# Expert weights fetched in whole halves again, the residual's home exchanged, and the combine weights turned large ones first

## What is computed

```
for layer in range(2):
    mix = ab_mixer(x) if layer == 0 else hgrn_mixer(x)
    x = layer_norm(ALPHA * x + mix)
    ff = moe(x, router_w, router_bias, w_gate[layer], w_up[layer], w_down[layer])
    x = layer_norm(ALPHA * x + ff)

def moe(h, ...):          # 16 experts in 4 groups of 4; each token takes 2 of one group
    ...
    for e in range(16):
        he = silu(t @ w_gate[e]) * (t @ w_up[e])         # 1024 -> 512
        y = y + gates[:, e:e + 1] * (he @ w_down[e])     # 512 -> 1024
```

## Time and profile before

| | us |
|---|---|
| median of 3 runs | 958.73 (956.76 to 959.33) |
| the profiled execution's own time | 956.18 |
| its span, first to last instruction | 954.4 |
| PE busy | 910.4 (95%) |
| MoE of layer 0, gate of quad 0 to the end of the last down | 303 to 516 |
| MoE of layer 1, the same | 725 to 936 |

### The profile page before, as it was taken

One profiled execution on the slowest core, in us unless ns is written; L12 is line 12 of the kernel. 1 busy time (PEld: TensorE's weight loads), 2 busy tenths in 40 slices (PEclk: granted clock), 3 DMA queues, 4 the chain that ended last, 5 costly groups with the idle time before them and its releaser, 6 DMA issues.

```text
span 954.4 us, 15651 instructions
## 1 busy us (share of the span) xinstructions
PE 910.4 (95%) x6463; PEld 560.7 (59%) x6463; DVE 370.7 (39%) x955; ACT 278.4 (29%) x591; POOL 103.6 (11%) x166
## 2 busy tenths in 40 slices
PE   9999999899999999999988899999999999999885
PEld 6777877686886353434324787777875444434223
DVE  2358876955317020111303336665346120203114
ACT  3534533222005020101002248887223201001003
POOL 2222121553000000000000001111300000000000
PEclk9999999999999999999999999999999999999988
DMA  9953353995985999999993954545798999999971
GB/s 378 352 234 138 139 199 132 394 376 192 423 365 207 376 370 420 421 419 420 422 421 141 384 234 161 183 185 200 285 425 311 411 386 420 421 421 421 420 314 47
DMA packets 41309, 299.84 MB, mean 314 GB/s; under 512 B 5065, under 2 KB 6601, under 8 KB 12809
## 3 DMA queue, kind: packets, MB, share of 16 engines
q1 hardware_dynamic: 36000, 268.52, 69.7%
q0 software_dynamic: 4544, 29.65, 8.1%
q10 hardware_dynamic: 688, 0.60, 0.2%
HBM read 283.32 MB, written 15.53 MB: 313 GB/s over the span
## 4 chain that ended last, share of the span: by engine, by line
PE 76%; DMA 11%; DVE 7%; ACT 2%; issue 2%; SPq 1%; POOL 1%; ACTq 0%; DVEq 0%; POOLq 0%
PE bank L1306 20%; PE bank L1344 11%; PE bank L1494 8%; PE bank L934 7%; PE bank L1181 6%; PE bank L1481 5%; PE bank L1370 3%; DMA ring<-in_w_down 3%; PE bank L1290 3%; DMA A<-in_w_down 3%; PE bank L1202 3%; DMA W<-in_conv_cols 1%; DVE ring L2209 1%; DMA spread<-xd_rows 1%; DMA spread<-v_rows 1%
## 5 line engine op out<-in xcount | busy, mean ns | idle before, releaser
L1306 PE MATMUL bank<-ring,W 128*32 128x512 f32 x1312 | 199.7, 608 | 9.4 <-DMA ring<-in_w_up 9.4
L934 PE MATMUL bank<-xT,ring 128*128 128x264 f32 x704 | 164.0, 389 | 1.3 <-DMA ring<-in_w_ab 1.2
L934 PEld LDWEIGHTS bank<-xT,ring 128*128 128x128 f32 x704 | 131.3, 190 | 31.0 <-issue 8.0
L1306 PE MATMUL bank<-A,W 128*32 128x512 f32 x544 | 125.6, 593 | 0.0
L1306 PEld LDWEIGHTS bank<-ring,W 128*32 128x32 f32 x1312 | 54.7, 112 | 106.9 <-issue 94.0
L1344 PE MATMUL bank<-ring,A 128*32 128x512 f32 x640 | 99.6, 599 | 0.0
L1344 PE MATMUL bank<-A 128*32 128x512 f32 x336 | 87.5, 621 | 2.8 <-DMA ring<-in_w_down 2.8
L2482 DVE TENSOR_TENSOR gkg<-gkg,bank 128x512 f32<-128x512 f32 x16 | 11.0, 688 | 186.1 <-PE bank L1306 186.1
L1494 PE MATMUL bank<-xT,ring 128*128 128x264 f32 x320 | 78.0, 391 | 0.0
L1494 PEld LDWEIGHTS bank<-xT,ring 128*128 128x128 f32 x320 | 58.3, 190 | 11.1 <-issue 1.6
L1306 PEld LDWEIGHTS bank<-A,W 128*32 128x32 f32 x544 | 32.9, 110 | 45.9 <-issue 45.5
(11 more groups left out here) (340 smaller groups left out, 1218.2 us busy)
## 6 DMA issues: line engine op xcount, KB each, us to landing
ring<-in_w_up SPq DMA_DIRECT2D x42, 1024.0 KB, 20.9
ring<-in_w_down SPq DMA_DIRECT2D x38, 1024.0 KB, 19.5
ring<-in_w_gate SPq DMA_DIRECT2D x34, 1024.0 KB, 15.8
ring<-in_w_ab SPq DMA_DIRECT2D x10, 2048.0 KB, 8.9
A<-in_w_gate SPq DMA_DIRECT2D x19, 1024.0 KB, 18.9
A<-in_w_down SPq DMA_DIRECT2D x16, 1024.0 KB, 23.9
ring<-in_w_c SPq DMA_DIRECT2D x8, 2048.0 KB, 11.0
A<-in_w_up SPq DMA_DIRECT2D x14, 1024.0 KB, 16.1
```

Source lines behind the costliest of these rows:

```text
L934: mm = pe.matmul(ab_bank(m)[:, 0:T], slot(AB_IN0 + m // 4, 8)[:, c, (m % 4) * P:(m % 4 + 1) * P], xT[:, c, :], start=(c == 0), stop=(c == ...
L1306: mm = pe.matmul(out[ROWS * g:ROWS * (g + 1), :], xg[:, c, E_G * b + g, :], w[g][:, c % 4, :], start=(c == 0), stop=(c == DC - 1))
```

## The change

Three edits. First, halves 20 to 27 are fetched whole, and PE goes through the gate of quad 0 as through every other: all four chunks of a half for block 0, then for block 1, and one mark at the end of each half. Second, home 18 now holds half 19 (down half 0 of quad 0) in place of half 14; half 14 goes to the home that half 16 had, 16 to that of 17, 17 to that of 18 and 18 to that of 19. The first fetches follow the homes' order as before. ACT therefore writes the residual after down half 0 has been read, between its two copies into `Y`. Third, `turn_weights` makes its eight large products one behind the other and then the eight small ones.

```diff
-        FIRST_ORDER = [[14, 15] + list(range(14)) + list(range(16, 20)),
-                       list(range(7)) + [14, 15] + list(range(7, 14)) + list(range(16, 20))]
+        FIRST_ORDER = [[19, 15] + list(range(15)) + list(range(16, 19)),
+                       list(range(7)) + [19, 15] + list(range(7, 15)) + list(range(16, 19))]
-        FIRST_HOMES = [r[:14] + [XACC_HOME, Y_HOME] + r[14:] for r in REST_HOMES]
+        FIRST_HOMES = [r[:15] + [Y_HOME] + r[15:] + [XACC_HOME] for r in REST_HOMES]
-        SPLIT_FILLS = 8
-        FILL_PARTS = [2 if FIRST <= 4 * n < FIRST + SPLIT_FILLS else 1 for n in range(MOE_HALVES // 4)]
-        READ_MARKS = MOE_HALVES // 4 + 2
+        READ_MARKS = MOE_HALVES // 4
...
-                for k0 in range(FIRST, MOE_HALVES, 4):
-                    parts = FILL_PARTS[k0 // 4]
-                    for part in range(parts):
-                        for k in range(k0, k0 + 4):
-                            before = max(m for m in range(k) if HOMES[layer][m] == HOMES[layer][k])
-                            sp.wait_ge(sem("moe_read"), half_read(layer, before, part if parts > 1 else 1))
-                            fill_part(layer, k, part, parts)
+                for k in range(FIRST, MOE_HALVES):
+                    before = max(m for m in range(k) if HOMES[layer][m] == HOMES[layer][k])
+                    sp.wait_ge(sem("moe_read"), half_read(layer, before))
+                    fill_half(layer, k)
...
-                        if q == i == 0:
-                            for part in range(2):
-                                for b in range(2):
-                                    if b == 1 and half == part == 0:
-                                        pe.wait_ge(sem("moe_slots"), 2 * layer + 2)
-                                    for c in range(4 * half + 2 * part, 4 * half + 2 * part + 2):
-                                        mm = product(b, c)
-                                mm.then_inc(sem("moe_read"), 1)
-                        else:
-                            for b in range(2):
-                                for c in range(4 * half, 4 * half + 4):
-                                    mm = product(b, c)
-                            mm.then_inc(sem("moe_read"), 1)
+                        for b in range(2):
...
+                            for c in range(4 * half, 4 * half + 4):
...
+                        mm.then_inc(sem("moe_read"), 1)
...
                 def turn_weights():
...
                     for r in range(2 * QUADS):
-                        out = bank[(4, 5, 2)[r // 3]][:, (r % 3) * SPREAD_N:(r % 3 + 1) * SPREAD_N]
-                        pe.transpose(out[:, 0:P], WS[:, r * P:(r + 1) * P], ident[:, :])
-                        tr = pe.transpose(out[:, P:SPREAD_N], WS2[:, r * P:(r + 1) * P], ident[0:NB, 0:NB])
+                        pe.transpose(turned[r][:, 0:P], WS[:, r * P:(r + 1) * P], ident[:, :])
+                    for r in range(2 * QUADS):
+                        tr = pe.transpose(turned[r][:, P:SPREAD_N], WS2[:, r * P:(r + 1) * P], ident[0:NB, 0:NB])
                     tr.then_inc(sem("pt_turned"), 1)
...
+                        if q == i == 0:
+                            act.wait_ge(sem("moe_read"), halves_read(layer, 0, 2, 0))
+                            act.activation(xacc[:, :, :], xT[:, :, :], ACT.Copy, scale=ALPHA).then_inc(sem("moe_residual"), 1)
...
-                    if q == 0:
-                        act.wait_ge(sem("moe_read"), halves_read(layer, 0, 1, 1))
-                        act.activation(xacc[:, :, :], xT[:, :, :], ACT.Copy, scale=ALPHA).then_inc(sem("moe_residual"), 1)
```

More of the change, by code:

```diff
@@ L239, in expert_ready, with halves_read, half_read @@
             n = 6 * q + 2 * i + half
-            parts = layer * sum(FILL_PARTS[n % FILLS::FILLS]) + sum(FILL_PARTS[n % FILLS:n + 1:FILLS])
-            eng.wait_ge(sem(f"moe_filled{n % FILLS}"), 64 * parts)
-        def halves_read(layer, q, i, half, part=1):
-            if q == i == 0:
-                return READ_MARKS * layer + 2 * half + part + 1
-            return READ_MARKS * layer + 6 * q + 2 * i + half + 3
-        def half_read(layer, k, part=1):
+            eng.wait_ge(sem(f"moe_filled{n % FILLS}"), 64 * (READ_MARKS // FILLS * layer + n // FILLS + 1))
+        def halves_read(layer, q, i, half):
+            return READ_MARKS * layer + 6 * q + 2 * i + half + 1
+        def half_read(layer, k):
             q, r = divmod(k, QUAD_HALVES)
-            return halves_read(layer, q, r // 8, r % 8 // 4, part)
+            return halves_read(layer, q, r // 8, r % 8 // 4)
         slot = chunks
@@ L408, in home_free, with fill_half @@
                 return [("heads_gated", 12), ("heads_prompt_state_stored0", 16 * 6), ("heads_prompt_state_stored1", 16 * 6)]
-            def fill_part(layer, k, part, parts):
+            def fill_half(layer, k):
                 q, r = divmod(k, QUAD_HALVES)
@@ L414, in fill_part @@
                 half, g = divmod(r, 4)
-                n, at = 6 * q + 2 * i + half, HALF_W // parts * part
                 src = expert_views(layer, bass.ds(E_G * g + q, 1))[i]
-                sp.dma_start(home_of(HOMES[layer][k])[:, at:at + HALF_W // parts],
-                             src[:, HALF_W * half + at:HALF_W * half + at + HALF_W // parts]).then_inc(
-                    sem(f"moe_filled{n % FILLS}"), 16)
+                sp.dma_start(home_of(HOMES[layer][k]), src[:, HALF_W * half:HALF_W * (half + 1)]).then_inc(
+                    sem(f"moe_filled{(6 * q + 2 * i + half) % FILLS}"), 16)
             def fill_first_expert(layer, k):
@@ L424, in fill_first_expert @@
                     sp.wait_ge(sem(name), value)
-                fill_part(layer, k, 0, 1)
+                fill_half(layer, k)
             def fill_experts(layer):
@@ L1299, in gate_up @@
                         w = [expert_half(layer, q, i, half, g) for g in range(E_G)]
-                        def product(b, c):
+                        for b in range(2):
                             out = up_bank(b) if i else gate_bank(b)
[L1303 to L1308, removed]
-                                mm.then_inc(sem("block_done"), 1)
-                            return mm
@@ L1312, in gate_up @@
-                        if q == i == 0:
-                            for part in range(2):
-                                for b in range(2):
-                                    if b == 1 and half == part == 0:
-                                        pe.wait_ge(sem("moe_slots"), 2 * layer + 2)
-                                    for c in range(4 * half + 2 * part, 4 * half + 2 * part + 2):
-                                        mm = product(b, c)
-                                mm.then_inc(sem("moe_read"), 1)
-                        else:
-                            for b in range(2):
-                                for c in range(4 * half, 4 * half + 4):
-                                    mm = product(b, c)
-                            mm.then_inc(sem("moe_read"), 1)
+                            if q == 0 and i == 0 and b == 1 and half == 0:
+                                pe.wait_ge(sem("moe_slots"), 2 * layer + 2)
@@ new lines, in gate_up @@
+                            for c in range(4 * half, 4 * half + 4):
+                                if i == 0 and b == 0 and c % 2 == 0:
+                                    pe.wait_ge(sem(f"xg_copied{c // 2 % 2}"), 2 * (L0 + q) + c // 4 + 1)
+                                for g in range(E_G):
+                                    mm = pe.matmul(out[ROWS * g:ROWS * (g + 1), :], xg[:, c, E_G * b + g, :], w[g][:, c % 4, :],
+                                                   start=(c == 0), stop=(c == DC - 1))
@@ L1326, in turn_hidden @@
+                            if b == 0 and half == 1:
+                                mm.then_inc(sem("block_done"), 1)
+                        mm.then_inc(sem("moe_read"), 1)
                 def turn_hidden(q, b):
@@ L1376, in turn_weights @@
                     pe.wait_ge(sem("moe_weighted"), layer + 1)
+                    turned = [bank[(4, 5, 2)[r // 3]][:, (r % 3) * SPREAD_N:(r % 3 + 1) * SPREAD_N] for r in range(2 * QUADS)]
                     for r in range(2 * QUADS):
-                        out = bank[(4, 5, 2)[r // 3]][:, (r % 3) * SPREAD_N:(r % 3 + 1) * SPREAD_N]
-                        pe.transpose(out[:, 0:P], WS[:, r * P:(r + 1) * P], ident[:, :])
-                        tr = pe.transpose(out[:, P:SPREAD_N], WS2[:, r * P:(r + 1) * P], ident[0:NB, 0:NB])
+                        pe.transpose(turned[r][:, 0:P], WS[:, r * P:(r + 1) * P], ident[:, :])
+                    for r in range(2 * QUADS):
+                        tr = pe.transpose(turned[r][:, P:SPREAD_N], WS2[:, r * P:(r + 1) * P], ident[0:NB, 0:NB])
                     tr.then_inc(sem("pt_turned"), 1)
```

## The result

The changed kernel took 952.4 us (median of 9, 948.32 to 955.62) against 957.15 us (9 runs, 955.77 to 959.64) of the kernel before: ratio 0.9949, interval [0.9929, 0.9968]. Part of that distance is the starting level: the prediction began from a median of 958.73 us (3 runs), and the same kernel measured 957.15 us over the 9 runs of this comparison. The profiled execution took 951.36 us, its span is 949.5 us.

What follows compares the result with a forecast made beforehand. Bound: the last weight fetch's landing in each MoE. Fetches and homes gave -2.7 (mean engine) to +0.7 us (slowest), taken as -1.5, the turn nothing: 954.7 from 956.18, median 957.2 us; range 953.3 to 962.0.

Steps and rivals of the forecast that it cites:

- whole fetches and homes: First two edits, at the fetch queue: later restart against closed second hole, net -1.95 us in layer 0, -0.77 in layer 1.
- The restart: Fetch queue starting again at half 20: 3.43 and 3.44 us later, winning back 2.37 and 2.15 us through whole fetches.
- the hole: Queue running low near down half 0 of quad 0: costs 3.01 us in layer 0, 2.06 in layer 1; new homes close it.
- half 42: Fetch waiting for quad 1's gate: a hole of a few tenths could open with PE late, none with PE 1.4 to 2.8 us earlier.
- the mean engine: Fetch gains reckoned by the mean rate of the DMA engines: together -2.7 us over both layers.
- the correction for the slowest engine: A half lands with its slowest DMA engine, which loses less in the hole: sum +0.7 us, so -1.5 us was taken.
- the third edit at nothing: Turned weights in quad 0 take 2.1 us in place of 3.50; PE is not the bound there, so worth nothing.
- the tail left out: Last 64 products of each MoE: forecast kept them at 8.81 us, against 6.94 us at full clock.
- theory P: From the experiments, on the last 64 products: waits ahead let the clock fall, and an early PE avoids it; up to 1.7 us per layer.
- Slow start whatever the size: Rival at the restart: idle time, not 4 KB rows, makes it slow; +1.8 to +5.2 us, middle 962.1 us, chance 0.2.
- The turn no shorter: Rival at the turned weights: no shortening, half 42 waits, up to 1.7 us in layer 0; 958.9 us, chance 0.05.
- The tail gains too: Faster rival: last 64 products avoid the low clock in one layer, -3.4 us, 955.3, or starts improve, -3 to -4; chance 0.25.

Runs made afterwards that it cites:

- e5: Kernel before plus 20 dummy products ahead of PE's wait for the last down half of quad 3: 958.09 against 956.35 us, ratio 1.0018.
- e6: Kernel before with the turned weights grouped, plus 10 dummy products ahead of PE's last wait: 951.67 against 956.35 us, ratio 0.9951.
- e4: Changed kernel with the turned weights alternating again, large and small: 954.19 against 956.53 us, ratio 0.9976 to the kernel before.
- e1: Kernel before with only the turned weights grouped, eight large then eight small: 950.29 against 956.53 us, ratio 0.9935.
- e14: Kernel before with only the turned weights grouped, third profile, timed beside the changed kernel: 952.27 against 956.56 us, ratio 0.9964.
- e11: Changed kernel with 14 dummy products behind the turned weights, holding PE back 3.3 us: 957.09 against 955.2 us, ratio 1.0009 to the kernel before.
- e3: Kernel before with only halves 20 to 27 fetched whole and quad 0's gate read by halves: 955.0 against 956.53 us, ratio 0.9988.
- e10: Kernel before plus 10 dummy products ahead of PE's wait for the last down half of quad 3: 954.4 against 955.2 us, ratio 0.9987.

## Why the prediction was wrong

**Right: what bounds the MoE.** In all 18 profiles PE reaches the last group before its weights have landed, but for three layers of e5 and e6 where dummy products filled the wait to the end and past it. The chain again leaves PE for the last fetches.

**Right in part: whole fetches and homes.** The restart came 3.4 us later after the gate, the rate behind it was 345 GB/s, the hole closed, half 42 found the queue busy. I had worked out -1.95 and -0.77 us for the mean engine. Measured over all profiles: 201.56 against 203.29 us, -1.73 us, and 201.27 against 202.03 us, -0.76 us. That looks like a hit, but all three edits are in it, and the turn alone closes the same hole. What the first two do without it stands in e4: -0.7 us in layer 1, as worked out; in layer 0, where the clock fell behind the turn, the start (204.26) is 0.7 us later than in the two layers 0 of before with the same fall (203.60). So the number for layer 0 came true only with the third edit.

**Wrong, the correction for the slowest engine.** "I take a value between -2.7 and +0.7, somewhat nearer to the mean engine". The stream gave 2.5 us. The correction had only one argument, a share of 0.12 in a window. In layer 1 its bound would have made e4's start later by 1.29 us, and it came 0.7 us sooner. Cost: 1.0 us of the miss.

**Wrong, the step that failed: the third edit at nothing.** "All of it lies in quad 0, where PE is not the bound: worth nothing by itself." Alone it is worth the whole gain (e1, e14), and taken out of the changed kernel it costs 2.6 us (e4: 954.79 against 952.17 us). What is then left of the gain, 956.39 - 954.79 = 1.6 us, is about the 1.5 us that I had put on the first two edits (2.3 us by e4's own ratio, 0.9976). I had found that SP waits at 347.32 for PE to read down half 0, and did not ask what it is worth if PE gets there earlier: PE is not the bound, yet its time sets the release, and the releases set the stream. e11 shows the same from the other side. The earlier PE was also mis-sized: the turn takes 1.61 us against 2.1, so at full clock down half 0 of quad 0 begins 1.7 us earlier (33.9 in place of 35.6 us after the gate) and not 1.4. And the fall of the clock behind the turn adds another 1.6 to 1.7 us of delay where it comes: the profiles show it in 7 of 18 layers with the alternating turn and in 0 of 18 with the grouped one.

**Wrong, a second step: the tail left out.** The forecast let the last 64 products take 8.81 us as before, and kept a lower figure for a rival of 0.25. In the profiles they took 8.77 us in 8 of 8 layers before and in 3 of 6 after: 1.70 x 2 x (1 - 0.5) = 1.7 us. With 2.5 us from the stream that is 4.2 us, as the means over all runs have it; with only 6 layers behind the half, so close an agreement is luck. The timed runs, each with its own granted clock, give a check. Their mean clock is 0.9867 before (104 runs) and 0.9889 in the changed kernel (21), and over all timed kernels a run is some 0.73 us shorter for each 0.001 of clock (a straight line laid through them). By that estimate 1.6 us of the gain go with the clock and 2.6 us stay at equal clock, much like tail and stream. (I had also read the cause loosely: the clock did not fall in the wait but at 507.50, 0.7 us into the group.) Why before always falls into it and the changed kernel half the time is not settled: theory P, a late PE, would have had e11 and e3 hit, and neither was (0 of 4), while e4 was (2 of 2). That the wait causes it is likely by e5, e10 and e6, and not shown, since e10 gained too little.

**The starting level.** The forecast of 957.2 stood on a median of 958.73 us, and the kernel before measured 957.15 us beside the changed one. So 1.6 of the 4.8 us between 957.2 and 952.4 belong to the level of three runs. Counted from its own start, the fast end of the range was -5.4 us, and -4.8 us was measured: as a difference it lay within the range, but only by the part that I had given to a rival.

**The rivals.** Slow start whatever the size: refuted, 345 GB/s. The turn no shorter: refuted. The tail gains too: this is what happened, in part.

## What to carry to other kernels

Where fetches wait for a reader to free their homes, an engine that is not the bound still sets the bound's pace: before pricing a shortcut on it at nothing, look whether a release that it gives is followed by a hole in the queue, and move that release. Close such a hole once: here three edits that close the same one were together worth no more than the smallest of them alone. And where an engine ends a phase by waiting, take the clock of the work behind the wait as a term of the sum of its own, and profile more than once before a single trace's value goes into it.

## What was not expected of the hardware

The restart of the idle fetch queue lost 9.31 x (1 - 266/420) = 3.41 us in its first 9.31 us with 512 KB fetches of 4 KB rows, and 9.31 x (1 - 345/420) = 1.66 us with 1 MiB fetches of 8 KB rows; e1, with parts again, had 267 GB/s, e3, with whole fetches, 347 GB/s. Behind the restart, in the 14 us to 330, mostly parts still, the queue moved 401 GB/s. Whether it is the size of the fetch or the length of its rows that counts, no run separates.

Eight large and eight small turned products took 3.31 us in alternation (16 of 18 layers; 3.41 and 3.50 us in the two where the clock fell before the end) and 1.61 us in two groups. That is 1.70 us for 14 changes between the two shapes fewer (not 15, as I had counted), an estimate of 0.12 us for each change. The Trainium skill ("TensorEngine Tiling (Array Packing)", Key Properties) says that a change of tiling mode drains the engine. The cost of a change agrees with that; that the two shapes run in different modes, no view of the profile shows. Dummy products of 128 columns, not turned, took 0.24 us each (20 in 4.73 us, in 40 records), where turned ones of the same shape take about 0.13 us (8 in 1.09 us): the trace shows two records for each dummy and one for each turned product.

In the kernel before, PE waited 2.5 to 3.1 us ahead of the last group, and the granted clock fell to 0.5 inside the group in 8 of 8 layers. The same wait was not enough each time: in the changed kernel the clock fell in 3 of 5 layers with waits of 2.7 to 2.9 us (a sixth waited 1.12 us and kept full clock), and in e1 it stayed at full after a wait of 3.05 us.
